# State-space table chunks beside layer 0's MLP: sixteen TensorE visits of one table, or eight of two

## The chip, the core and the metric

The program runs on one core of one Trainium2 chip. The metric is the device time of one execution in microseconds (us). TensorE (PE in the profile) multiplies, VectorE (DVE) and ScalarE (ACT) do the elementwise work, GpSimd (POOL) some more of it, and SyncE (SP) issues the weight loads as DMAs. ScalarE and GpSimd issue DMAs too. The engines run their own instruction streams and meet only at semaphores: a wait holds back everything behind it in the same stream.

## What is computed

A decoder trunk of two layers over 256 tokens of width 2048, all in float32: each layer has a mixer, a cross-attention and an MLP. Layer 1's mixer holds a state-space part, whose step for one group is, in the reference:

```python
lam = lax.complex(jnp.minimum(a_re, -1e-4), a_im)
a_bar = jnp.exp(lam * step)
b_bar = ((a_bar - 1.0) / lam)[..., None] * lax.complex(b_re, b_im)
bu = jnp.einsum('blgc,gpc->blgp', uf, b_bar)
states = associative_scan(combine, (a_seq, bu))      # x_t = a_bar x_(t-1) + bu_t
y = jnp.einsum('blgp,gcp->blgc', states, c_mat).real + d_skip * uf
...
ff = sq_relu_mlp(x, w1, w2)                          # square(relu(x @ w1)) @ w2
```

The kernel turns the scan into chunks of 8 tokens. For that it needs tables that depend on the weights alone: powers of a_bar times b_bar ("E"), c times powers of a_bar ("C"), and the product of both, an 8-token convolution kernel ("K") to which d_skip is added. The 64 groups are made in 16 tables of four groups each, k = 0 to 15, and since they need no activations they are made long before layer 1, beside layer 0's MLP.

## The kernel before

**The MLP.** Layer 0's MLP goes through its 8192 hidden columns in eight steps of 1024. One step is 32 "halves": u = 0 and 1 make the hidden columns (w1), u = 2 and 3 are pair units that multiply them with w2, eight halves i = 0 to 7 each. For a half, ScalarE rounds a slab of weights to whi (L1484), VectorE takes the remainder wlo = raw - whi (L2128), and TensorE multiplies both. whi and wlo are rings of four halves: ScalarE's whi of half t waits until TensorE is done with half t - 4. In the pair units and at the start of the next step VectorE also adds finished blocks to the residual h (add_block, L2176), which is what frees an accumulator bank. TensorE's first half of a next step opens a bank that is freed by the add_block in VectorE's slot i = 1 of that same step.

**The slots of the tables.** The last but one four steps (TAB_CHUNKS) carry the table work. Slots count halves, t = 0 to 127 (32 per step); the slot of half t stands in each stream after that half's own work. For table k, before:

- SP loads its factors at slot 28 + 6k of SP's own stream, behind a wait for the builders of table k - 2.
- VectorE makes the real parts in the four slots from DVE_T[k] = 30 + 6k (L2236 to L2255), and raises s5_re. GpSimd makes the imaginary parts (tt, L3059, and L3277), and raises s5_im. Buffers etab, cz and eb are double (k % 2): a builder of table k waits until table k - 2 has been multiplied and stored.
- TensorE visits at CHUNK_T[k] = 33 + 6k: s5_chunk(k) is four small float32 products (stationary 32 columns, moving 128) into one of the two banks of "at" (L827). The profile shows each visit as eight matmuls.
- ScalarE's slot is four later, 37 + 6k: copy the bank's lower half into ksb (L1594), issue the stores of E (et_d, L1596) and C (ca_d, two of them, L1599), wait for VectorE's two adds (k_sum; VectorE: L2214 and L2217, behind k_part), issue two stores of ksb (k_d, L1602). Then whi of the next half follows.

There is one ksb only: the copy of table k (L1594) waits for k_out, the landing of both k_d stores of table k - 1. At the end GpSimd waits for the last k_out and issues the t_d copies (L3285).

Of the kernel before, what the change touches and what calls it, by code (L numbers as in the profile page):

```python
# [27 lines left out]
ACT = mybir.ActivationFunctionType  # L28
# [3 lines left out]
P = 128  # L32
# [12 lines left out]
G, GC, ST = 64, 16, 64  # L45
# [3 lines left out]
GW = T8 * GC  # L49
# [86 lines left out]
def trunk(nc, x, mem, norm_final, ab_w_in, ab_b_forget,  # L136
# [3 lines left out]
    with ctx:  # L140
# [3 lines left out]
        def sem(name):  # L144
            return ctx.enter_context(nc.semaphore(name))
# [27 lines left out]
        def view(at, n, pattern=None, p=P, **sizes):  # L173
            assert at + n <= A_SIZE
            a = arena[0:p, at:at + n]
            return a.rearrange(pattern, **sizes) if pattern else a
# [12 lines left out]
        etab = view(1024, 1024, "p (b q r w) -> p b q r w", b=2, q=2, r=2)  # L189
# [5 lines left out]
        ksb = view(3200, 240, p=2 * 2 * GC)  # L195
# [7 lines left out]
        cz = [view(at_, 576, "p (q r w) -> p q r w", q=2, r=2) for at_ in (7616, 10240)]  # L203
# [70 lines left out]
        at = ctx.enter_context(nc.psum_tensor("at", [P, 2, NB], F32))  # L274
# [3 lines left out]
        et_d = nc.dram_tensor("et_d", [P, Q, 2, GW], F32, kind="Internal").ap()  # L278
        ca_d = nc.dram_tensor("ca_d", [2, P, Q, GW], F32, kind="Internal").ap()
        k_d = nc.dram_tensor("k_d", [GC, G, 240], F32, kind="Internal").ap()  # L280
# [18 lines left out]
        at_full = sem("at_full")  # L299
# [28 lines left out]
        s5_re, s5_im = sem("s5_re"), sem("s5_im")  # L328
        s5_used = sem("s5_used")
        k_part, k_sum = sem("k_part"), sem("k_sum")  # L330
        f_out, f_in = sem("f_out"), [sem(f"f_in{b}") for b in range(2)]
        et_out, k_out = [sem(f"et_out{b}") for b in range(2)], sem("k_out")
        ca_out = [sem(f"ca_out{b}") for b in range(2)]
        prep_done, tab_zero = sem("prep_done"), sem("tab_zero")
        ksb_zero = sem("ksb_zero")
# [28 lines left out]
        OUT_ORDER = (2, 3, 0, 1)  # L364
        TAB_CHUNKS = (3, 4, 5, 6)
        FACTOR_T, STORE_T = 4, 16
        DVE_T = [32 + 6 * k - 2 for k in range(16)]
        CHUNK_T = [32 + 6 * k + 1 for k in range(16)]
        SIN_T = 29
        X8_T, SCAN_T, Y_T = 25, 39, 53  # L370
        SWAP_T = (49, 51, 52)
# [5 lines left out]
        at_before_tab = at_before_factors + 1  # L377
# [317 lines left out]
        def _(pe):  # L695
            p = Place()
# [119 lines left out]
            def open_at():  # L816
                n = p.n.setdefault("at", 0)
                if n >= 2:
                    pe.wait_ge(at_free[n % 2], n // 2)
                return at[:, n % 2, :]  # L820

            def close_at(last):
                last.then_inc(at_full, 1)
                p.bump("at")

            def mm(o, lhsT, rhs, start=True, stop=True):
                return pe.matmul(o, lhsT, rhs, start=start, stop=stop)  # L827
# [13 lines left out]
            def s5_factors():  # L841

                assert p.n["at"] == at_before_factors
                pe.wait_ge(prep_done, 1)
                bank = open_at()
                for t in range(2):
                    for r in range(2):
                        last = pe.transpose(bank[:, (2 * t + r) * P:(2 * t + r + 1) * P],
                                            pb[:, r, 4 * t:4 * t + 4, :].rearrange("p a b -> p (a b)"), ident[:, :])
                close_at(last)  # L850

            def s5_chunk(k):

                b = k % 2
                pe.wait_ge(s5_re, k + 1)
                pe.wait_ge(s5_im, k + 1)
                bank = open_at()
                for r in range(2):
                    for q in range(2):
                        ln = 2 * GC * (2 * r + q)  # L860
                        last = mm(bank[ln:ln + 2 * GC, 0:GW], eb[:, b, q, r, :], cz[b][:, q, r, 0:GW])
                close_at(last)

            def s5_tables(t):
                if t == FACTOR_T:
                    s5_factors()
                if t in CHUNK_T:
                    assert p.n["at"] == at_before_tab + CHUNK_T.index(t)
                    s5_chunk(CHUNK_T.index(t))

            for u in range(4):
                def after(i, u=u):
# [589 lines left out]
        def _(act):  # L1462
            p = Place()
# [119 lines left out]
            def s5_tables(t):  # L1583

                if t - 4 == FACTOR_T:
                    at_copy(lambda bank: [(fput, bank)])
                if t - 4 not in CHUNK_T:
                    return
                k = CHUNK_T.index(t - 4)
                b = k % 2  # L1590
                n = p.n["at"]
                act.wait_ge(*((k_out, 32 * k) if k else (ksb_zero, 1)))
                act.wait_ge(at_full, n + 1)
                act.activation(ksb[:, 112:240], at[2 * 2 * GC:P, n % 2, 0:GW], ACT.Copy).then_inc(k_part, 1)  # L1594
                p.bump("at")
                act.dma_start(et_d[:, 2 * k:2 * k + 2].rearrange("p q r w -> p (q r w)"),  # L1596
                              etab[:, b].rearrange("p q r w -> p (q r w)")).then_inc(et_out[b], 16)
                for r in range(2):
                    act.dma_start(ca_d[r, :, 2 * k:2 * k + 2], cz[b][:, :, r, GC:]).then_inc(ca_out[b], 16)  # L1599
                act.wait_ge(k_sum, k + 1)  # L1600
                for q in range(2):
                    act.dma_start(k_d.rearrange("c (s k q) w -> k q s c w", s=2, q=2)[k, q],  # L1602
                                  ksb[2 * GC * q:2 * GC * (q + 1), :]).then_inc(k_out, 16)

            for u in range(4):
                def slot(i, u=u):
# [503 lines left out]
        def _(dve):  # L2110
            dve.memset(idle[:, :], 0.0).then_inc(idle_set, 1)
            p = Place()
# [94 lines left out]

            def re_tables(t):

                if t - 4 in CHUNK_T:  # L2210
                    k = CHUNK_T.index(t - 4)
                    n = at_before_tab + k
                    dve.wait_ge(k_part, k + 1)
                    dve.tensor_tensor(ksb[:, 112:240], at[0:2 * 2 * GC, n % 2, 0:GW], ksb[:, 112:240],  # L2214
                                      ALU.add).then_inc(at_free[n % 2], 1)
                    dve.wait_ge(at_free[n % 2], n // 2 + 1)
                    dve.tensor_tensor(ksb[:, 112:112 + GC], ksb[:, 112:112 + GC], skip[:, k, :],  # L2217
                                      ALU.add).then_inc(k_sum, 1)
                part = [(k, t - t0) for k, t0 in enumerate(DVE_T) if 0 <= t - t0 < 4]
                if not part:  # L2220
                    return
                (k, part), = part
                b, q0 = k % 2, 2 * k
                e, tv = etab[:, b, :, 0, :], vtmp3[:, 0:2 * P].rearrange("p (q w) -> p q w", q=2)
                t1 = vtmp2.rearrange("p (q i c) -> p q i c", q=2, i=9)
                t2 = vtmp.rearrange("p (q i c) -> p q i c", q=2, i=9)
                if part == 0:
                    if k == 0:
                        dve.wait_ge(prep_done, 1)
                        dve.wait_ge(tab_zero, 1)  # L2230
                    if k >= 2:
                        dve.wait_ge(at_full, at_before_tab + k - 1)
                        dve.wait_ge(et_out[b], 16 * (k // 2))
                    dve.wait_ge(f_in[b], 32 * (k // 2 + 1))
                    (br, bi), (pbr, pbi) = ((fac[:, b, f, :, r, :] for r in range(2)) for f in range(2))
                    dve.tensor_tensor(e, br, pbr, ALU.mult)  # L2236
                    dve.tensor_tensor(tv, bi, pbi, ALU.mult)
                    (br, bi), (pbr, pbi) = last_parts(q0)
                    dve.tensor_tensor(vlast[:, 0], br, pbr, ALU.mult)
                    link(dve.tensor_tensor(vlast[:, 1], bi, pbi, ALU.mult))  # L2240
                elif part == 1:
                    dve.tensor_tensor(e, e, tv, ALU.subtract)
                    for s in range(2):
                        ln = slice(64 * s, 64 * s + 64)
                        last = dve.tensor_tensor(eb[ln, b, :, 0, s * GC:(s + 1) * GC], vlast[ln, 0], vlast[ln, 1],
                                                 ALU.subtract)
                    link(last)
                elif part == 2:
                    cr, ci, pr_, pi_ = table_parts(s5c, pw, q0, 9)
                    dve.tensor_tensor(t1, cr, pr_, ALU.mult)  # L2250
                    link(dve.tensor_tensor(t2, ci, pi_, ALU.mult))
                else:
                    if k >= 2:
                        dve.wait_ge(ca_out[b], 32 * (k // 2))
                    dve.tensor_tensor(cz[b][:, :, 0, :].rearrange("p q (i c) -> p q i c", i=9), t1, t2, ALU.add)\  # L2255
                       .then_inc(s5_re, 1)
# [1121 lines left out]
```

## Time and profile before

| | us |
|---|---|
| median of 3 runs | 2376.73 (2376.65 to 2376.74) |
| the profiled execution | 2375.98 |
| its span, first to last instruction | 2374.1 |
| TensorE busy | 2361.8 (99%) |
| VectorE, ScalarE, GpSimd busy | 1643.4, 1234.3, 346.3 |
| first and last table visit of TensorE | 948.48, 1205.59 |

A busy TensorE is not one at its peak: its matmuls overlap, so the distance between two starts tells more than a duration. In the tables' steps an ordinary matmul of 512 columns starts 0.225 to 0.23 us after the one before it, and is shown as lasting 0.39.

### The profile page before, as it was taken

What the parts mean: (1) busy time and instruction counts of PE and PEld (TensorE: products, weight loads), DVE (VectorE), ACT (ScalarE), POOL (GpSimd) and SP (SyncE); (2) the same over time, 40 slices, a digit from 0 to 9 for tenths busy, and PEclk for the clock granted to TensorE, in tenths of its full rate; (3) what the DMA queues carried; (4) which work ended last, traced back from release to release, by engine and by line L of the source; (5) the groups of instructions that cost most, each with busy time, mean ns of one, the idle gap of its engine ahead of it and who ended that gap; (6) DMA issues with size and microseconds to landing.
All of it is one profiled execution on the core that took longest, in us unless ns stands there. A gap on an engine that the chain in (4) does not pass through costs nothing.

```text
span 2374.1 us, 31055 instructions
## 1 busy us (share of the span) xinstructions
PE 2361.8 (99%) x12350; PEld 1997.7 (84%) x12350; DVE 1643.4 (69%) x2041; ACT 1234.3 (52%) x1629; POOL 346.3 (15%) x469
## 2 busy tenths in 40 slices
PE   9999999999999999999999999999999999999998
PEld 7888888889888888888888888889888888888887
DVE  5546555556655557888866647566688888888886
ACT  7544445546544444444445445556656555555554
POOL 0033120002264002455510100000000000000001
PEclk9999999999999999999999999999999999999999
DMA  9755564564656566788785768955656756756653
GB/s 357 264 173 188 170 218 163 184 188 145 195 179 198 191 198 212 247 243 253 243 284 186 214 231 237 296 200 155 225 183 220 234 168 221 239 185 205 230 160 142
DMA packets 345082, 499.89 MB, mean 211 GB/s; under 512 B 18904, under 2 KB 184640, under 8 KB 344688
## 3 DMA queue, kind: packets, MB, share of 16 engines
q1 hardware_dynamic: 319792, 471.37, 61.8%
q0 software_dynamic: 3888, 14.02, 1.9%
q10 hardware_dynamic: 21264, 12.59, 1.7%
q8 instruction: 95, 1.56, 0.3%
q14 instruction: 43, 0.35, 0.0%
HBM read 483.06 MB, written 19.08 MB: 212 GB/s over the span
## 4 chain that ended last, share of the span: by engine, by line
PE 95%; DVE 2%; ACT 1%; DMA 1%; issue 0%; ACTq 0%; SPq 0%; DVEq 0%
PE acc L740 15%; PE acc L742 15%; PE acc L741 15%; PE acc L1177 10%; PE acc L1386 9%; PE acc L1185 5%; PE acc L1395 5%; PE acc L1426 2%; PE acc L1425 2%; PE acc L1424 2%; PE at L827 2%; PE tp L803 1%; PE at L1366 1%; PE at L1368 1%; PE at L1369 1%; DVE wlo L2128 1%
## 5 line engine op out<-in xcount | busy, mean ns | idle before, releaser
L2128 DVE TENSOR_TENSOR wlo<-raw,whi 128x1024 fp32r<-128x1024 f32 x592 | 763.1, 1296 | 538.7 <-ACT whi L1484 535.9
L1484 ACT ACTIVATE whi<-raw 128x1024 fp32r<-128x1024 f32 x600 | 630.5, 1059 | 660.6 <-PE acc L742 395.1
L740 PE MATMUL acc<-whi,yt_hi 128*128 128x512 f32 x960 | 378.2, 394 | 0.3 <-DVE h L2176 0.3
L742 PE MATMUL acc<-whi,yt_lo 128*128 128x512 f32 x960 | 374.0, 390 | 0.0
L741 PE MATMUL acc<-wlo,yt_hi 128*128 128x512 f32 x960 | 373.7, 389 | 0.0
L2884 DVE TENSOR_TENSOR wlo<-raw,whi 128x1024 fp32r<-128x1024 f32 x176 | 214.3, 1221 | 80.3 <-ACT whi L2041 74.5
L2041 ACT ACTIVATE whi<-raw 128x1024 fp32r<-128x1024 f32 x168 | 176.0, 1056 | 174.5 <-PE acc L1395 85.6
L740 PE MATMUL acc<-whi,x 128*128 128x512 f32 x672 | 265.8, 396 | 0.0
L1177 PE MATMUL acc<-x,whi 128*128 128x512 f32 x1088 | 262.4, 391 | 0.0
L742 PE MATMUL acc<-whi,x 128*128 128x512 f32 x672 | 261.9, 390 | 0.0
L741 PE MATMUL acc<-wlo,x 128*128 128x512 f32 x672 | 261.7, 389 | 0.0
L3059 POOL TENSOR_TENSOR arena<-arena 128x32 f32<-128x32 f32 (+5 forms) x275 | 197.2, 717 | 357.3 <-DMA arena<-fp_d 179.1
L1177 PEld LDWEIGHTS acc<-x,whi 128*128 128x128 f32 x1088 | 199.6, 188 | 39.3 <-issue 0.8
L740 PEld LDWEIGHTS acc<-whi,yt_hi 128*128 128x128 f32 x960 | 180.3, 188 | 39.3 <-issue 1.8
L1386 PE MATMUL acc<-x,whi 128*128 128x512 f32 x896 | 213.0, 390 | 0.0
L742 PEld LDWEIGHTS acc<-whi,yt_lo 128*128 128x128 f32 x960 | 180.2, 188 | 37.9
L741 PEld LDWEIGHTS acc<-wlo,yt_hi 128*128 128x128 f32 x960 | 180.3, 188 | 36.3
L1386 PEld LDWEIGHTS acc<-x,whi 128*128 128x128 f32 x896 | 166.4, 188 | 33.4
L2030 ACT ACTIVATE whi<-arena 128x1024 fp32r<-128x1024 f32 x98 | 103.2, 1060 | 90.9 <-PE acc L1426 35.0
L740 PEld LDWEIGHTS acc<-whi,x 128*128 128x128 f32 x672 | 126.2, 188 | 26.6 <-issue 1.2
L742 PEld LDWEIGHTS acc<-whi,x 128*128 128x128 f32 x672 | 126.1, 188 | 26.7
L741 PEld LDWEIGHTS acc<-wlo,x 128*128 128x128 f32 x672 | 126.3, 188 | 25.2
(274 smaller groups left out, 3184.6 us busy)
## 6 DMA issues: line engine op xcount, KB each, us to landing
raw<-in_mlp_w SPq DMA_DIRECT2D x228, 1024.0 KB, 5.8
raw<-in_ab_w_in SPq DMA_DIRECT2D x56, 1024.0 KB, 5.1
arena<-in_mlp_w SPq DMA_DIRECT2D x35, 1024.0 KB, 6.5
raw<-in_cd_w_in SPq DMA_DIRECT2D x32, 1024.0 KB, 5.9
raw<-in_ab_w_out SPq DMA_DIRECT2D x16, 1024.0 KB, 5.0
raw<-in_cd_w_out SPq DMA_DIRECT2D x16, 1024.0 KB, 8.3
raw<-in_xa_wkv SPq DMA_DIRECT2D x14, 1024.0 KB, 11.7
raw<-in_xa_wq SPq DMA_DIRECT2D x16, 512.0 KB, 4.5
```

Of the source, the lines that this page charges most:

```text
L740: pe.matmul(a, xh, whi[:, w, kk], start=opens and kk == 0, stop=False)
L741: pe.matmul(a, xh, wlo[:, w, kk], start=False, stop=False)
L742: last = pe.matmul(a, xl, whi[:, w, kk], start=False, stop=closes and kk == 1)
L1177: last = pe.matmul(head(i).rearrange("p (a n) -> p a n", a=2), split_weights(whi, "heads", i)[:, kk, :], x2[:, :, k0 + kk, :], start=i < 4 ...
L1185: last = pe.matmul(head(i)[:, 0:L], split_weights(wlo, "heads", i)[:, kk, :], x2[:, 0, 8 * (i // 4) + kk, :], start=False, stop=i >= 4 and ...
L1386: last = pe.matmul(head(i).rearrange("p (a n) -> p a n", a=2), split_weights(whi, "heads", p.n["half"] + i % 2)[:, kk, :], x2[:, :, 8 * (i ...
L1395: last = pe.matmul(head(i)[:, 0:L], split_weights(wlo, "heads", p.n["half"] + i % 2)[:, kk, :], x2[:, 0, 8 * (i // 4) + kk, :], start=Fals ...
L1484: act.activation(split_weights(whi, kind, p.n["half"] + i), half_weights(raw, kind, i), ACT.Copy)\
L2041: act.activation(split_weights(whi, kind, p.n["half"]), half_weights(raw, kind, i), ACT.Copy)\
L2128: dve.tensor_tensor(split_weights(wlo, kind, n), half_weights(raw, kind, i), split_weights(whi, kind, n).bitcast(F32), ALU.subtract).then_ ...
L2884: dve.tensor_tensor(split_weights(wlo, kind, n), half_weights(raw, kind, i), split_weights(whi, kind, n).bitcast(F32), ALU.subtract).then_ ...
L3059: link(pool.tensor_tensor(o, a, b, op))
```

## The change

TensorE visits eight times instead of sixteen (VISIT_T = 39 + 12v), with tables 2v and 2v + 1 in one visit, at the slot where table 2v + 1 had its own. VectorE's parts of an even table from 2 on start one slot later. ScalarE's stores of E and C keep their slots (37 + 6k), but now wait for the two builders (s5_re, s5_im) instead of for TensorE. The copy, the sums and the k_d stores of a pair (SUM_T) stand at slots 43 + 12v and 45 + 12v, cut off at 127: for the last pair both are 127. GpSimd and SP keep their order.

```diff
--- before.py
+++ after.py
@@ -364,8 +364,10 @@
         OUT_ORDER = (2, 3, 0, 1)
         TAB_CHUNKS = (3, 4, 5, 6)
         FACTOR_T, STORE_T = 4, 16
-        DVE_T = [32 + 6 * k - 2 for k in range(16)]
-        CHUNK_T = [32 + 6 * k + 1 for k in range(16)]
+        DVE_T = [32 + 6 * k - 2 + (k > 0 and k % 2 == 0) for k in range(16)]
+        STORE_TABLE_T = [32 + 6 * k + 5 for k in range(16)]
+        VISIT_T = [32 + 12 * v + 7 for v in range(8)]
+        SUM_T = [min(VISIT_T[k // 2] + 4 + 2 * (k % 2), 127) for k in range(16)]
         SIN_T = 29
         X8_T, SCAN_T, Y_T = 25, 39, 53
         SWAP_T = (49, 51, 52)
@@ -864,9 +866,11 @@
             def s5_tables(t):
                 if t == FACTOR_T:
                     s5_factors()
-                if t in CHUNK_T:
-                    assert p.n["at"] == at_before_tab + CHUNK_T.index(t)
-                    s5_chunk(CHUNK_T.index(t))
+                if t in VISIT_T:
+                    v = VISIT_T.index(t)
+                    assert p.n["at"] == at_before_tab + 2 * v
+                    s5_chunk(2 * v)
+                    s5_chunk(2 * v + 1)
 
             for u in range(4):
                 def after(i, u=u):
@@ -1584,23 +1588,25 @@
 
                 if t - 4 == FACTOR_T:
                     at_copy(lambda bank: [(fput, bank)])
-                if t - 4 not in CHUNK_T:
-                    return
-                k = CHUNK_T.index(t - 4)
-                b = k % 2
-                n = p.n["at"]
-                act.wait_ge(*((k_out, 32 * k) if k else (ksb_zero, 1)))
-                act.wait_ge(at_full, n + 1)
-                act.activation(ksb[:, 112:240], at[2 * 2 * GC:P, n % 2, 0:GW], ACT.Copy).then_inc(k_part, 1)
-                p.bump("at")
-                act.dma_start(et_d[:, 2 * k:2 * k + 2].rearrange("p q r w -> p (q r w)"),
-                              etab[:, b].rearrange("p q r w -> p (q r w)")).then_inc(et_out[b], 16)
-                for r in range(2):
-                    act.dma_start(ca_d[r, :, 2 * k:2 * k + 2], cz[b][:, :, r, GC:]).then_inc(ca_out[b], 16)
-                act.wait_ge(k_sum, k + 1)
-                for q in range(2):
-                    act.dma_start(k_d.rearrange("c (s k q) w -> k q s c w", s=2, q=2)[k, q],
-                                  ksb[2 * GC * q:2 * GC * (q + 1), :]).then_inc(k_out, 16)
+                if t in STORE_TABLE_T:
+                    k = STORE_TABLE_T.index(t)
+                    b = k % 2
+                    act.wait_ge(s5_re, k + 1)
+                    act.wait_ge(s5_im, k + 1)
+                    act.dma_start(et_d[:, 2 * k:2 * k + 2].rearrange("p q r w -> p (q r w)"),
+                                  etab[:, b].rearrange("p q r w -> p (q r w)")).then_inc(et_out[b], 16)
+                    for r in range(2):
+                        act.dma_start(ca_d[r, :, 2 * k:2 * k + 2], cz[b][:, :, r, GC:]).then_inc(ca_out[b], 16)
+                for k in (k for k in range(16) if SUM_T[k] == t):
+                    n = p.n["at"]
+                    act.wait_ge(*((k_out, 32 * k) if k else (ksb_zero, 1)))
+                    act.wait_ge(at_full, n + 1)
+                    act.activation(ksb[:, 112:240], at[2 * 2 * GC:P, n % 2, 0:GW], ACT.Copy).then_inc(k_part, 1)
+                    p.bump("at")
+                    act.wait_ge(k_sum, k + 1)
+                    for q in range(2):
+                        act.dma_start(k_d.rearrange("c (s k q) w -> k q s c w", s=2, q=2)[k, q],
+                                      ksb[2 * GC * q:2 * GC * (q + 1), :]).then_inc(k_out, 16)
 
             for u in range(4):
                 def slot(i, u=u):
@@ -2207,8 +2213,7 @@
 
             def re_tables(t):
 
-                if t - 4 in CHUNK_T:
-                    k = CHUNK_T.index(t - 4)
+                for k in (k for k in range(16) if SUM_T[k] == t):
                     n = at_before_tab + k
                     dve.wait_ge(k_part, k + 1)
                     dve.tensor_tensor(ksb[:, 112:240], at[0:2 * 2 * GC, n % 2, 0:GW], ksb[:, 112:240],
```

On TensorE, at the first two tables (L827 is the helper mm of before; L740 to L742, L1177 and L1185 are the MLP's), before:

```order
L1185 MATMUL acc<-x,wlo 128x256 x8
L827 MATMUL at<-arena 32x128 x4
L1177 MATMUL acc<-x,whi 128x512 x8
L1185 MATMUL acc<-x,wlo 128x256 x8
L1177 MATMUL acc<-x,whi 128x512 x8
L1185 MATMUL acc<-x,wlo 128x256 x16
L1177 MATMUL acc<-x,whi 128x512 x16
L1185 MATMUL acc<-x,wlo 128x256 x16
L1177 MATMUL acc<-x,whi 128x512 x16
L1185 MATMUL acc<-x,wlo 128x256 x8
L827 MATMUL at<-arena 32x128 x4
L1177 MATMUL acc<-x,whi 128x512 x8
```

and now (the same lines carry numbers 2 to 4 higher, mm is L829):

```order
L1189 MATMUL acc<-x,wlo 128x256 x8
L1181 MATMUL acc<-x,whi 128x512 x8
L1189 MATMUL acc<-x,wlo 128x256 x8
L1181 MATMUL acc<-x,whi 128x512 x8
L1189 MATMUL acc<-x,wlo 128x256 x16
L1181 MATMUL acc<-x,whi 128x512 x16
L1189 MATMUL acc<-x,wlo 128x256 x16
L1181 MATMUL acc<-x,whi 128x512 x16
L1189 MATMUL acc<-x,wlo 128x256 x8
L829 MATMUL at<-arena 32x128 x8
L1181 MATMUL acc<-x,whi 128x512 x8
```

Table 0's four products have moved 6 halves down to table 1's, and are one row of eight with them.

On ScalarE, at the last table of all and the start of the next step, before (with what each row waits for):

```order
L1484 ACTIVATE whi<-raw 128x1024 [waits half_used,raw_landed3]
L1484 ACTIVATE whi<-raw 128x1024 [waits half_used]
L1594 ACTIVATE arena<-at 64x128 [waits at_full,k_out]
L1596 DMA et_d<-arena 128x512
L1599 DMA ca_d<-arena 128x2x128 x2
L1602 DMA k_d<-arena 2x16x240 [waits k_sum]
L1602 DMA k_d<-arena 2x16x240
L1484 ACTIVATE whi<-raw 128x1024 [waits half_used,raw_landed0]
L1484 ACTIVATE whi<-raw 128x1024 [waits half_used]
```

and now (L1484 is L1488, L1594 is L1604, L1602 is L1608):

```order
L1488 ACTIVATE whi<-raw 128x1024 [waits half_used]
L1596 DMA et_d<-arena 128x512 [waits s5_im,s5_re]
L1599 DMA ca_d<-arena 128x2x128 x2
L1604 ACTIVATE arena<-at 64x128 [waits at_full,k_out]
L1608 DMA k_d<-arena 2x16x240 [waits k_sum]
L1608 DMA k_d<-arena 2x16x240
L1604 ACTIVATE arena<-at 64x128 [waits at_full,k_out]
L1608 DMA k_d<-arena 2x16x240 [waits k_sum]
L1608 DMA k_d<-arena 2x16x240
L1488 ACTIVATE whi<-raw 128x1024 [waits half_used,raw_landed0]
L1488 ACTIVATE whi<-raw 128x1024 [waits half_used]
```

Between whi of half 127 and whi of half 128 there is now a second copy of a bank, which waits for k_out, with a second pair of k_d stores.

On VectorE at the same place, before (L2214 and L2217 are the sums, L2176 is add_block):

```order
L2128 TENSOR_TENSOR wlo<-raw,whi 128x1024 [waits hi_ready] x4
L2214 TENSOR_TENSOR arena<-at,arena 64x128 [waits k_part]
L2217 TENSOR_TENSOR arena<-arena 64x16 [waits at_free1]
L2128 TENSOR_TENSOR wlo<-raw,whi 128x1024 [waits hi_ready] x2
L2176 SCALAR_TENSOR_TENSOR h<-acc,rstd,h 128x512 [waits half_used]
L2176 SCALAR_TENSOR_TENSOR h<-acc,rstd,h 128x512
L2128 TENSOR_TENSOR wlo<-raw,whi 128x1024 [waits hi_ready]
```

and now (L2128 is L2134, L2176 is L2182):

```order
L2134 TENSOR_TENSOR wlo<-raw,whi 128x1024 [waits hi_ready] x4
L2219 TENSOR_TENSOR arena<-at,arena 64x128 [waits k_part]
L2222 TENSOR_TENSOR arena<-arena 64x16 [waits at_free0]
L2219 TENSOR_TENSOR arena<-at,arena 64x128 [waits k_part]
L2222 TENSOR_TENSOR arena<-arena 64x16 [waits at_free1]
L2134 TENSOR_TENSOR wlo<-raw,whi 128x1024 [waits hi_ready] x2
L2182 SCALAR_TENSOR_TENSOR h<-acc,rstd,h 128x512 [waits half_used]
L2182 SCALAR_TENSOR_TENSOR h<-acc,rstd,h 128x512
L2134 TENSOR_TENSOR wlo<-raw,whi 128x1024 [waits hi_ready]
```

Both pairs of sums stand ahead of wlo of halves 128 and 129, and of the add_block behind them.

## Rows read from the trace of the kernel before

**Rows 1.** The page: the engines' busy time and share of the span.

```profile
PE 2361.8 (99%) x12350; PEld 1997.7 (84%) x12350; DVE 1643.4 (69%) x2041; ACT 1234.3 (52%) x1629; POOL 346.3 (15%) x469
```

**Rows 2.** Waits of TensorE, whole run: waiter, releaser, us in total, times, longest.

```profile
PE acc L740 <- DVE h L2176: 0.3, 1, 0.3
```

**Rows 3.** Timeline, TensorE, last visit: start, us, engine, line, out<-in, count.

```profile
1205.28 0.39 PE L742 MATMUL acc<-whi,yt_lo 128*128 128x512 f32 x1
1205.59 0.43 PE L827 MATMUL at<-arena 128*32 128x128 f32 x8
1205.95 0.50 PE L740 MATMUL acc<-whi,yt_hi 128*128 128x512 f32 x1
1206.29 0.39 PE L741 MATMUL acc<-wlo,yt_hi 128*128 128x512 f32 x1
```

**Rows 4.** Timeline, TensorE, a visit of layer 1 with four such groups.

```profile
1467.02 0.39 PE L742 MATMUL acc<-whi,x 128*128 128x512 f32 x1
1467.34 0.48 PE L827 MATMUL at<-yt_hi,arena 128*32 128x128 f32 x8
...
1468.41 0.50 PE L740 MATMUL acc<-whi,x 128*128 128x512 f32 x1
1468.75 0.40 PE L741 MATMUL acc<-wlo,x 128*128 128x512 f32 x1
```

**Rows 5.** Timeline, TensorE, halves 56 and 58, then the start of the next step.

```profile
1011.89 0.50 PE L740 MATMUL acc<-whi,yt_hi 128*128 128x512 f32 x1 [0.30 <-DVE h L2176]
...
1017.59 0.42 PE L827 MATMUL at<-arena 128*32 128x128 f32 x8
...
1216.98 3.79 PE L1177 MATMUL acc<-x,whi 128*128 128x512 f32 x16
```

**Rows 6.** Timeline, ScalarE, slot 127 (last table) to half 129; ACTq issues DMAs.

```profile
1205.70 1.06 ACT L1484 ACTIVATE whi<-raw 128x1024 fp32r<-128x1024 f32 x1 [1.60 <-PE acc L742]
...
1206.66 0.26 ACT L1594 ACTIVATE arena<-at 64x128 f32<-64x128 f32 x1
...
1208.44 1.20 ACTq L1602 DMA_DIRECT2D k_d<-arena  x2
1209.74 1.06 ACT L1484 ACTIVATE whi<-raw 128x1024 fp32r<-128x1024 f32 x1 [2.82 <-PE acc L742]
```

**Rows 7.** Timeline, VectorE, the same stretch: sums, wlo of half 128, add_block.

```profile
1207.94 0.28 DVE L2214 TENSOR_TENSOR arena<-at,arena 64x128 f32<-64x128 f32 x1
1208.25 0.17 DVE L2217 TENSOR_TENSOR arena<-arena 64x16 f32<-64x16 f32 x1
1210.84 1.22 DVE L2128 TENSOR_TENSOR wlo<-raw,whi 128x1024 fp32r<-128x1024 f32 x1 [2.42 <-ACT whi L1484]
...
1213.98 1.40 DVE L2176 SCALAR_TENSOR_TENSOR h<-acc,rstd,h 128x512 f32<-128x512 f32 x2
```

**Rows 8.** Timeline, GpSimd: the end of a table, and t_d behind the last k_out.

```profile
1178.88 10.10 POOL L3059 TENSOR_TENSOR arena<-arena 128x256 f32<-128x256 f32 x9 [5.86 <-DMA ca_d<-arena]
1189.06 0.89 POOL L3277 TENSOR_TENSOR arena<-arena 128x288 f32<-128x288 f32 x1
1216.37 6.17 POOL L3285 DMA_DIRECT2D t_d<-k_d  x8 [26.42 <-DMA k_d<-arena]
```

**Rows 9.** The view of the tile ca_d: its DMAs, issue to landing.

```profile
DMA to landing us min/median/max: 3.4/6.4/10.1
```

**Rows 10.** Timeline, TensorE's last matmul of the program.

```profile
2365.08 0.39 PE L764 MATMUL acc<-whi,yt_lo 128*128 128x512 f32 x1
```

**Rows 11.** Windows behind it: PE, PEld, DVE, ACT, POOL busy (count), PEclk, DMA.

```profile
2368.00:2370.00 2.00, 0.00 (x0) 0.00 (x0) 1.69 (x4) 1.15 (x1) 0.00 (x0) 0.95 0.00 0
2370.00:2372.00 2.00, 0.00 (x0) 0.00 (x0) 0.00 (x0) 0.00 (x0) 0.00 (x0) 0.50 0.72 297
```

**Rows 12.** Windows, L827 at the program's start: PE busy (count), PEld busy (count).

```profile
1.20:3.20 2.00, 2.00 (x5) 0.90 (x6) 1.00 0.60 166
3.20:5.20 2.00, 2.00 (x8) 0.92 (x7) 1.00 1.05 389
```

## The prediction

> **What bounds the kernel.** I read the page first: TensorE is busy for 99% of the span [rows 1]. Then the view of waits, for TensorE alone: in the steps with table work it waits once, 0.3 us, for an add_block of VectorE [rows 2], and the timeline puts that at the start of half 56 [rows 5]. So a change can only act in three ways: through what a table visit costs on TensorE itself, through that one wait, or by making VectorE or ScalarE late enough to stop TensorE. For the last I read, engine by engine, the place where the order changed most: the last table, slot 127.
>
> **Visits merged: a gain.** Starts of ordinary matmuls are 0.227 us apart. Round the last visit the starts run 1205.28, 1205.59, 1205.95, 1206.29 [rows 3]: 1.01 us where two ordinary distances take 0.45, so a visit of one table costs 0.56. How much of that is per visit and how much per table no table visit shows, but layer 1's visits do, with four groups of the same shape: 1467.02 to 1468.75 is 1.73 [rows 4], less 0.45 is 1.28. Each further group adds (1.28 - 0.56) / 3 = 0.24. A pair in one visit then costs 0.80 instead of 1.12, and eight pairs save 8 x 0.32 = **2.5 us**. If the second table cost its whole inner distance of 0.36, it would be 8 x 0.20 = 1.6. If it cost 0.22 (the inner distance left if the longer first and last ones are set apart), 2.7. I take 2.5, since the four-group visit holds the same waits and the same change of bank. All of it is on the path, because TensorE waits for nothing else.
>
> **VectorE one slot later for even tables: 0.3 gained.** The 0.3 us before half 56 come from the sums of table 3 and the parts of table 4 standing ahead of an add_block. Part 0 of table 4 (the longest) moves behind slot 54, the wlo of half 56 comes earlier, and the wait should go. Bound 0, I take **0.3**.
>
> **The last visit: a loss.** The pairs' sums are two slots apart, except the last pair's, whose two stand in slot 127. There is one ksb, so the second copy waits until the first k_d stores have landed, and behind it on ScalarE's stream stands whi of half 128. Worked out with the rows of the same place:
> - The first k_d pair is issued at 1208.44 for 1.20, to 1209.64 [rows 6]. It doesn't come earlier or later than before, since VectorE's sums at 1207.94 follow its wlo [rows 7].
> - Landing: GpSimd's t_d copies, which wait for the same semaphore, start at 1216.37 [rows 8], so 6.7 after the issue ended at most. By the ca_d stores' median of 6.4 from the issue [rows 9], the second store (issued some 0.6 before 1209.64) lands at 1215.4. I take 1215.9, between the two.
> - Then copy 0.26 [rows 6], sums 0.48 (1207.94 to 1208.42 [rows 7]), stores 1.20, and some 0.2 in hand-overs: whi of half 128 starts at 1218.04 instead of 1209.74 [rows 6].
> - VectorE's wlo starts 1.10 behind it [rows 6, 7]: 1219.1. Two wlo (1.22 each) and the add_block (1.40) [rows 7] end at 1222.9. Before, that add_block ended at 1215.38.
> - TensorE's half 128 needs this add_block's bank. It started at 1216.98 [rows 5]; a visit longer by 0.24 makes it 1217.2. The cover before was 1.6 us, now TensorE stands still for 1222.9 - 1217.2 = **5.7 us**.
>
> The unknown is the landing. With the least of a store's landings, 3.4, it is 1212.4 and the stall 2.2. With the most, 10.1, it is 1219.1 and the stall 8.9 [rows 9].
>
> **The clock: a loss on top.** A stall of that length is new to this trace. What it does to the clock is bounded by the program's two ends. After the last matmul ends at 2365.47 [rows 10], the granted clock is 1.00, then 0.95 in 2368 to 2370, then 0.50 [rows 11]: 0.95 is 0.1 x 2 us at half rate, so it fell from 2.4 to 1.2 GHz at 2369.8, 4.3 us after TensorE had stopped. A stop of 5.7 is longer. At the start 5 matmuls lie in the first 2 us and 8 in the next 2 [rows 12]; with 0.43 us each at first and half of it later, the low rate lasts for 3.2 us of work and loses 1.6. The bounds are 0 and twice that. I take **1.6**. The Trainium skill's page "TensorE: Matmul & The Clock Gate", Part 1, has the same rule, throttled by default and released by sustained activity; by the end of this trace it agrees, and no row shows a fall in mid-kernel.
>
> **Edits taken at nothing.** The odd table of a pair other than the last: its copy comes two slots after the even one's stores. From the visit: 4.05 to the end of the k_d issue (1205.59 to 1209.64), 6.3 to land, 1.9 for copy, sums and stores, then 1.06, 1.22 and 1.40 for the next half and its block. That is 16.0, and TensorE comes to that bank after a 0.8 visit and six halves of 12 x 0.227, 17.1. So 1 us of cover at slots 57, 81 and 105, where a block is handed over, and more elsewhere; VectorE's table parts there can eat it. I take 0, bound 3 x 1.2. GpSimd now starts both tables of a pair behind one visit: a table lasts 11.1 (1178.88 to 1189.95 [rows 8]), two 22, and visits are 12 halves apart. 66 halves lie between 1017.59 and 1205.59 [rows 3, 5], 2.85 each, so 34 us. ScalarE's new wait for the builders comes 6 halves, 17 us, behind the visit that frees an even table's buffers, where its builder needs some 12; the odd one has 34 for 23. SP's factor load of the next even table comes about 11 us behind it, so SP may wait up to 1 us ahead of weight loads that are issued eight halves early. Both at 0.
>
> **Sum.** -2.5 - 0.3 + 5.7 + 1.6 = +4.5 us. The profiled execution of 2375.98 would take 2380.5; the median lies 0.75 above it, so 2376.73 + 4.5 = **2381.2**.
>
> **The rivals.**
> - *The stall without the fall of the clock.* The sum without 1.6 is +2.9, 2379.6. For it: the stop is only 1.4 us longer than the 4.3 us after which the clock fell [rows 10, 11], and a landing 1.5 us sooner undoes it.
> - *The k_d stores land quickly, and the change is faster than before.* They are 30 KB each behind a few larger stores. It decides at a stall of 2.8, that is a landing at 1213.0, 3.4 after the issue. With the least landing [rows 9] the sum is -2.5 - 0.3 + 2.2 = -0.6, 2376.1. Against it: this very store took until close to 1216.37 [rows 8]. The Trainium skill's page "DMA: Bandwidth & Descriptors", Anatomy of one DMA, gives some 2 us of fixed cost and next to nothing for so few bytes; by it the stall would be about 0.9 and the time 2374.8, but the trace doesn't agree (3.4 is its least).
> - *Longer landings, or VectorE late in the middle too.* Landing 10.1 makes the sum +7.7, and the three places with 1 us of cover add up to 3.6 where landings are long: 2385 and over.
>
> **How the numbers follow.** Forecast 0.50, stall without clock 0.28, quick landing 0.10, long 0.12. The range, 2377.5 to 2385.0, takes in the first two with their bounds and half of each of the others. A measurement of this kernel tells about 0.2%, 4.75 us: slower means over 2381.5. A good 0.4 of the forecast's cases lie above it (0.22), half the clock-less ones' upper bound reaches it (0.06), and the long ones do (0.12): slower 0.40. Faster than 2372.0 needs a gain no term holds: 0.02. The rest, 0.58, is no change.
>
> **What would show it.** Right: TensorE has one long idle time, before half 128 at about 1217, ended by VectorE's h (L2182), with the second copy (L1604) and its k_d stores some 8 us behind the first; a granted clock below 1 for a few us behind it; eight visits of 16 matmuls costing 0.80. Wrong: no idle time there (the landing is quicker), idle time at halves 58, 82 or 106, ScalarE waiting for GpSimd ahead of et_d, or visits that cost 1.1.

## The result

| | before | changed | |
|---|---|---|---|
| median | 2376.37 us (9 runs, 2375.07 to 2376.93) | 2383.58 us (9 runs, 2383.19 to 2384.50) | ratio 1.0029 [1.002, 1.0037] |
| span of the profiled execution | 2374.1 | 2382.4 | |

The changed kernel is 7.2 us slower, 0.3%. By the prediction's own line of 2381.5 that is slower, to which it gave 0.40; it held no change to be likelier (0.58). The first view to read is again that of TensorE's waits, of the changed kernel (its add_block is L2182, its sums of hidden columns are L2518); in [rows 2] there was one line for these steps:

```profile
PE acc L1181 <- DVE h L2182: 5.9, 2, 5.4
PE acc L712 <- ACT whi L1488: 1.5, 2, 1.3
...
PE acc L742 <- DVE h L2182: 1.0, 1, 1.0
PE acc L742 <- DVE arena L2518: 0.8, 1, 0.8
```

One wait of 5.4 us is new, and three short ones (0.46, 0.98 and 0.84). The L712 line is the start of the program and not of the change: another profile of the same kernel (the run called "the changed kernel again" below) shows 0.3 there. It matters only for the two profiled spans: a matmul that starts at 15.76 before starts at 16.75 here, so 1.0 of the 8.3 us between the spans lies there, and 7.3 remain. TensorE's timeline, at the last visit and at the start of the next step (it answers to [rows 3] and the last of [rows 5]):

```profile
1205.88 0.39 PE L744 MATMUL acc<-whi,yt_lo 128*128 128x512 f32 x1
1206.20 0.65 PE L829 MATMUL at<-arena 128*32 128x128 f32 x16
1206.77 0.50 PE L742 MATMUL acc<-whi,yt_hi 128*128 128x512 f32 x1
1207.11 0.40 PE L743 MATMUL acc<-wlo,yt_hi 128*128 128x512 f32 x1
...
1217.57 0.39 PE L744 MATMUL acc<-whi,yt_lo 128*128 128x512 f32 x1
1223.38 5.74 PE L1181 MATMUL acc<-x,whi 128*128 128x512 f32 x16 [5.42 <-DVE h L2182]
```

A visit of two tables takes 1.23 us from start to start where two ordinary distances take 0.45: 0.78. The first matmuls behind the stop take 5.74 us for sixteen, 3.79 before [rows 5]. Why TensorE stops, read from the bottom up: the timelines of ScalarE and of VectorE in the same kernel (they answer to [rows 6] and [rows 7]).

```profile
1209.05 1.20 ACTq L1608 DMA_DIRECT2D k_d<-arena  x2
1216.44 0.28 ACT L1604 ACTIVATE arena<-at 64x128 f32<-64x128 f32 x1 [8.27 <-DMA k_d<-arena]
1217.27 1.19 ACTq L1608 DMA_DIRECT2D k_d<-arena  x2
1218.56 3.90 ACT L1488 ACTIVATE whi<-raw 128x1024 fp32r<-128x1024 f32 x4 [1.84 <-PE acc L744]
```

```profile
1216.75 0.28 DVE L2219 TENSOR_TENSOR arena<-at,arena 64x128 f32<-64x128 f32 x1 [7.74 <-ACT arena L1604]
1217.07 0.17 DVE L2222 TENSOR_TENSOR arena<-arena 64x16 f32<-64x16 f32 x1
1219.65 2.36 DVE L2134 TENSOR_TENSOR wlo<-raw,whi 128x1024 fp32r<-128x1024 f32 x2 [2.41 <-ACT whi L1488]
1221.92 1.40 DVE L2182 SCALAR_TENSOR_TENSOR h<-acc,rstd,h 128x512 f32<-128x512 f32 x2
```

The add_block ends at 1223.32, TensorE starts at 1223.38. It waited for two wlo, they for whi, whi for the second pair of k_d stores, those for the sums, the sums for the second copy, and the copy for table 14's stores: it starts 6.2 us after their issue ended at 1210.25, so they had landed by then.

The windows of the changed kernel show the clock (columns: PE, PEld, DVE, ACT, POOL busy, the granted clock, the DMA share and GB/s):

```profile
1216.00:1219.00 3.00, 1.96 (x9) 1.30 (x7) 0.45 (x2) 0.72 (x2) 0.00 (x0) 1.00 0.02 6
1219.00:1222.00 3.00, 0.00 (x0) 0.00 (x0) 2.35 (x3) 3.00 (x4) 1.05 (x2) 0.74 0.04 15
1222.00:1225.00 3.00, 1.62 (x4) 1.33 (x5) 3.00 (x5) 0.45 (x1) 3.00 (x5) 0.50 0.81 233
1225.00:1228.00 3.00, 3.00 (x10) 2.38 (x9) 1.91 (x3) 0.00 (x0) 2.13 (x3) 0.62 0.90 243
1228.00:1231.00 3.00, 3.00 (x22) 2.79 (x21) 0.00 (x0) 0.83 (x1) 0.00 (x0) 1.00 1.04 391
```

0.74 over 3 us is 1.56 us at half rate, so the clock fell from 2.4 to 1.2 GHz at 1220.4, 2.5 us after the last matmul's end. 0.62 is 2.28 us, so it rose at 1227.3, 3.9 us after TensorE had taken up work. That is 1.95 us lost, 5.74 less 3.79. These figures are one execution's. In the second profile of this kernel the windows put the fall 4.0 us after the last matmul's end and the rise 5.6 us after the restart, and the same sixteen matmuls take 6.54 us: 2.75 lost.

### The profile page after: what moved, and what is told of

The parts are those of the page before. It is cut to its first block, busy times and chain, and to the rows that moved or that the text cites. A ratio compares the mean times of both kernels' runs of the same rounds, so it can differ in the third digit from the quotient of the medians.

```text
span 2382.4 us, 31071 instructions
## 1 busy us (share of the span) xinstructions
PE 2362.2 (99%) x12350; PEld 1999.8 (84%) x12350; DVE 1629.1 (68%) x2041; ACT 1235.0 (52%) x1629; POOL 335.5 (14%) x469
## 3 DMA queue, kind: packets, MB, share of 16 engines
q8 instruction: 95, 1.56, 0.3%
## 4 chain that ended last, share of the span: by engine, by line
PE 93%; DVE 3%; ACT 2%; DMA 1%; issue 1%; ACTq 0%; SPq 0%; DVEq 0%
PE acc L742 15%; PE acc L744 14%; PE acc L743 14%; PE acc L1181 10%; PE acc L1390 9%; PE acc L1189 5%; PE acc L1399 4%; PE acc L1428 2%; PE acc L1429 2%; PE acc L1430 2%; PE at L829 2%; PE tp L805 1%; PE at L1370 1%; PE at L1372 1%; PE at L1373 1%; DVE wlo L2134 1%
## 5 line engine op out<-in xcount | busy, mean ns | idle before, releaser
L2134 DVE TENSOR_TENSOR wlo<-raw,whi 128x1024 fp32r<-128x1024 f32 x592 | 752.2, 1277 | 548.4 <-ACT whi L1488 545.6
L1488 ACT ACTIVATE whi<-raw 128x1024 fp32r<-128x1024 f32 x600 | 630.0, 1058 | 638.7 <-PE acc L744 401.1
L742 PE MATMUL acc<-whi,yt_hi 128*128 128x512 f32 x960 | 377.8, 394 | 1.8 <-DVE h L2182 1.0
L2889 DVE TENSOR_TENSOR wlo<-raw,whi 128x1024 fp32r<-128x1024 f32 x176 | 214.2, 1221 | 80.3 <-ACT whi L2047 74.5
L742 PE MATMUL acc<-whi,x 128*128 128x512 f32 x672 | 265.8, 396 | 0.0
L3064 POOL TENSOR_TENSOR arena<-arena 128x32 f32<-128x32 f32 (+5 forms) x275 | 178.8, 650 | 368.9 <-DMA arena<-fp_d 179.0
L742 PEld LDWEIGHTS acc<-whi,yt_hi 128*128 128x128 f32 x960 | 180.3, 188 | 40.1 <-DVE h L2182 1.4
L742 PEld LDWEIGHTS acc<-whi,x 128*128 128x128 f32 x672 | 126.2, 188 | 26.5 <-issue 1.2
```

The source lines that it names most:

```text
L742: pe.matmul(a, xh, whi[:, w, kk], start=opens and kk == 0, stop=False)
L1488: act.activation(split_weights(whi, kind, p.n["half"] + i), half_weights(raw, kind, i), ACT.Copy)\
L2134: dve.tensor_tensor(split_weights(wlo, kind, n), half_weights(raw, kind, i), split_weights(whi, kind, n).bitcast(F32), ALU.subtract).then_ ...
L2889: dve.tensor_tensor(split_weights(wlo, kind, n), half_weights(raw, kind, i), split_weights(whi, kind, n).bitcast(F32), ALU.subtract).then_ ...
L3064: link(pool.tensor_tensor(o, a, b, op))
```

## The experiments

Two theories for the end: **L**, the last landing stops TensorE and the stop lowers the clock; **S**, two rounds of copy, sums and stores are too much for slot 127 whatever lands when. For the three short waits: the landings again, or **R**, the round trip between ScalarE and VectorE. Twelve runs, each beside runs of the kernel before on the same chip. The medians of these lie from 2376.8 to 2377.7, and all their single runs but one (2434.3) from 2375.0 to 2380.8; most versions spread less, so differences between the versions are tighter than those against the kernel before. "Under the changed kernel" is against its 2383.58; measured again, on the chip of two of the versions, it gave 2383.43.

**A second ksb for the last table alone.**

```diff
-        ksb = view(3200, 240, p=2 * 2 * GC)
+        ksbs = [view(at_, 240, p=2 * 2 * GC) for at_ in (3200, 3936)]
...
-                    n = p.n["at"]
-                    act.wait_ge(*((k_out, 32 * k) if k else (ksb_zero, 1)))
+                    n, ksb = p.n["at"], ksbs[k == 15]
+                    act.wait_ge(*((k_out, 32 * k) if 0 < k < 15 else (ksb_zero, 1)))
```

> The changed kernel, but table 15 (the last) has a ksb of its own, so its copy does not wait for the landing of table 14's k_d stores; all other tables share one ksb as in the change. Theory L (the last landing stops TensorE, and the stop lowers the clock): the idle time before half 128 (5.4 us in the changed kernel) and the 3.9 us of work at half the clock (2 us lost) both go, the three short waits at halves 48, 96 and 120 stay: about 7.4 us faster than the changed kernel, within 1 us of the kernel before. Rival S (ScalarE and VectorE are late at slot 127 because of two rounds of copy, sums and stores, whatever the landing): the idle time shrinks by 1 to 2 us only.

2375.77 us, ratio 0.9995 [0.9986, 1.0004] to before: 7.8 under the changed kernel. (One of its twelve executions took 13593.9 us, for a reason that the record doesn't show; the others took 2375.3 to 2376.7.) TensorE has no idle time at half 128 and the granted clock stays at 1.00; the three short waits stand (0.46, 0.83, 0.98). L holds, S falls: two rounds in one slot are covered.

**Two ksb, for all tables** (`ksbs[k % 2]`, and `k_outs[k % 2]` with 32 * (k // 2)).

> The changed kernel with two ksb, one for even and one for odd tables, each with its own landing semaphore: no copy waits for the stores of its own pair. Theory L for the end as in the run with a second ksb for table 15 only. For the short waits at halves 48, 96 and 120 two theories: if the landings make ScalarE late there too, they go, and the time is 2.5 to 3 us under the kernel before; if it is the second round of copy, sums and stores two slots after the first (ScalarE waiting for VectorE's sums), they stay, and the time is that of the run with a second ksb for table 15 only.

2375.15, ratio 0.9994 [0.9985, 1.0003], and again beside later runs:

> The version with two ksb as before, again, to stand beside the one with later stores on the same chip: 1 to 2 us under the kernel before, waits of 0.83 and 0.98 us at halves 48 and 120.

2375.44, ratio 0.9992 [0.9983, 1.0001]. The waits at halves 48 and 120 stay at 0.83 and 0.98, the one at 96 goes. So the landings made the one, and something else the other two: the expectation had them all go or all stay.

**The changed kernel again**, in the same session.

> The changed kernel itself on the same chip: 7 us over the kernel before, 8.5 over the version with two ksb.

2383.43, ratio 1.0027 [1.0018, 1.0036], idle time 5.1 before half 128: the result repeats. The clock's part does so only roughly, as said above (2.75 us lost against 1.95).

**TensorE kept busy during the stop.**

```diff
+                if t == 127:
+                    pe.wait_ge(at_free[0], (at_before_tab + 14) // 2 + 1)
+                    for _ in range(12):
+                        mm(at[0:32, 0, 0:L], ident[:, 0:32], idle)
```

> The changed kernel with 12 extra small products of TensorE (24 matmul records of 0.215 us, 5.2 us in all) between half 127 and half 128, into a bank nobody reads, in the time in which it stands idle. If the idle time is what lowers the clock, TensorE stays at 2.4 GHz, the first sixteen matmuls of half 128 take 3.8 us instead of 5.7, and the whole is about 2 us faster than the changed kernel. If the clock falls for another reason, the time is that of the changed kernel. If the filling itself runs past the release, up to 0.5 us are lost.

2381.10, ratio 1.0019 [1.001, 1.0028]: 2.5 under the changed kernel. Its timeline, TensorE:

```profile
1216.78 5.37 PE L829 MATMUL at<-arena,ident 128*32 128x256 f32 x24
1222.11 3.96 PE L1185 MATMUL acc<-x,whi 128*128 128x512 f32 x16
```

Half 128 still begins 5.4 us late, since its bank comes no sooner, but its sixteen matmuls take 3.96 instead of 5.74 or 6.54, at a granted clock of 1.00. So the idle time itself lowered the clock, and products that nobody reads buy it back. The 2.5 us lie between the two clock losses seen.

**Stores of E and C behind the k_d stores in slot 127** (the block of stores is moved below the sums' loop for t == 127).

> The changed kernel, but in slot 127 the three stores of table 15 (E and C, 512 KB) are issued behind the two copies, sums and k_d stores instead of ahead of them. In the changed kernel k_d stores with such stores just ahead on the same queue land 5.2 to 6.2 us after their issue, those without after 2.9 to 3.8. If the stores ahead make the landing long, table 14's lands about 3 us sooner and is issued up to 0.5 sooner, but the three stores then stand between it and whi of half 128 (1.4 us): idle time about 3.5 instead of 5.4, and with no fall of the clock or a shorter one: 2 to 4 us faster than the changed kernel. If the landing is long because of the weight loads, the time is 1 us slower than the changed kernel.

2385.44, ratio 1.0035 [1.0022, 1.0048]: 1.9 over the changed kernel. ScalarE's timeline:

```profile
1208.06 1.21 ACTq L1611 DMA_DIRECT2D k_d<-arena  x2
1215.19 0.27 ACT L1607 ACTIVATE arena<-at 64x128 f32<-64x128 f32 x1 [8.65 <-DMA k_d<-arena]
```

The issue ends at 1209.27, the copy starts 5.9 later. The stores ahead on the queue are not what makes the landing long. They only move in front of whi, and the idle time grows to 6.7. My first guess was wrong here. The DMA view by short stretches shows what the landing waits for, since only the k_d stores are on ScalarE's queue in this run: between 1209.3 and 1212.8 that queue moves no packet and SyncE's moves 896, of the weight load; the k_d packets run from 1213.2 to 1214.8, and the load's last ones end by 1213.4. In the changed kernel they run from 1214.4 to 1216.0, with most of the load through by 1214.5. The clock is at 1.2 GHz here too: it falls 2.7 us after the last matmul's end and rises 2.8 us after the restart, and the sixteen matmuls take 5.24 us, 1.45 lost.

**One weight load cut to an eighth**, the one issued 0.4 us ahead of the k_d stores. This version leaves out seven eighths of that load, so it computes something else and only its time counts.

```diff
...
+                        rows = 128 if cut and i == 3 else 1024
-                        sp.dma_start(raw[:, i].rearrange("p a (b n) -> p (a b) n", b=2),
+                        sp.dma_start(raw[:, i].rearrange("p a (b n) -> p (a b) n", b=2)[:, 0:rows // 128],
...
```

> The changed kernel, but one weight load, that for halves 134 and 135 (issued 0.5 us ahead of table 14's k_d stores, 1 MB, landing 0.6 us ahead of them), brings only its first 128 of 1024 rows, so part of layer 0's MLP is computed with stale weights. If the k_d stores land late because they queue behind this load's packets, table 14's land 2.5 to 3.5 us after their issue instead of 6.2, the idle time before half 128 is 2 to 3 us instead of 5.4, the clock does not fall, and the time is 4.5 to 5.5 us under the changed kernel. If a store with nothing but itself takes that long, nothing changes.

2377.65, ratio 1.0006 [0.9996, 1.0015]: 5.9 under the changed kernel. ScalarE and then TensorE:

```profile
1207.87 1.21 ACTq L1609 DMA_DIRECT2D k_d<-arena  x2
1211.25 0.28 ACT L1605 ACTIVATE arena<-at 64x128 f32<-64x128 f32 x1 [4.29 <-DMA k_d<-arena]
```

```profile
1218.20 3.96 PE L1182 MATMUL acc<-x,whi 128*128 128x512 f32 x16 [1.42 <-DVE h L2183]
```

The copy comes 2.2 us after the issue's end instead of 6.2, the idle time is 1.4 and the clock stays at 1.00. With the packets of the run before this one: a store of 30 KB lands no sooner than the megabyte of weights that was issued just ahead of it on another queue. By what order the packets of the two queues are served, no run shows.

**Both sums of a pair in one slot**, with two ksb: both copies, both sums, then four k_d stores behind one wait.

> The version with two ksb, and the two sums of every pair in one slot (43 + 12v): ScalarE copies both banks, VectorE makes both sums, then ScalarE issues the four k_d stores; one wait for VectorE per pair instead of two. Theory R (the waits at halves 48 and 120 come from the second round of copy and sums two slots after the first): they go, 1.8 us of idle time, and the time is about 2 us under the version with two ksb alone, 3.5 to 4 us under the kernel before. Rival V (they come from VectorE having table parts to do there anyway): they stay, and nothing changes against two ksb alone.

2376.34, ratio 0.9999 [0.999, 1.0008], 1.2 over two ksb alone, so neither theory's forecast came. The waits at halves 48 and 120 shrink to 0.35 and 0.60, but three others come, at 56, 80 and 104 (0.61, 0.53, 0.52), as the timeline reads because ScalarE now issues four stores in one piece:

```profile
1004.37 2.43 ACTq L1610 DMA_DIRECT2D k_d<-arena  x4
1006.90 2.02 ACT L1488 ACTIVATE whi<-raw 128x1024 fp32r<-128x1024 f32 x2 [3.32 <-issue]
```

R as I put it, the second round alone, falls: one long block of ScalarE's stream is as bad as two short ones.

**The same without VectorE's shift** (`DVE_T = [32 + 6 * k - 2 for k in range(16)]`).

> The same with VectorE's parts of even tables at the slots of the kernel before (30 + 6k), so without the shift by one slot. If the shift is what took the 0.3 us wait at half 56 away, it comes back here, and VectorE waits 1 to 2 us more for TensorE's visit at the start of an even table. If the wait went for another reason, the time is that of the version with one round, within 0.5 us.

2384.28, ratio 1.0031 [1.0019, 1.0042], 7.9 over the version with the shift. TensorE waits three times, where a bank's owner comes late, and VectorE waits three times for TensorE's visit (2.3 us in all, about as expected). What was not expected is the price:

```profile
PE acc L742 <- DVE h L2184: 2.6, 1, 2.6
PE acc L742 <- DVE arena L2520: 1.7, 1, 1.7
PE acc L1181 <- DVE arena L2520: 1.7, 1, 1.7
```

The 0.3 us that I gave the shift is far too little here: with two sums in slot 43 + 12v, part 0 of the next table one slot ahead of them costs 1.7 to 2.6 us at each of halves 56, 80 and 104. These waits make some 4 of the 7.9 us (its profiled span is 2379.7 against 2376.2). The profiled execution is one of the fast ones: the three of seven executions with a mean granted clock of 0.999 took 2381.4 to 2382.1, and the four with 0.997 or 0.998 took 2384.3 to 2385.8. So in those four the clock probably falls as well; where, no profile shows.

**The other half of the change alone**: the kernel before, sixteen visits, stores ahead of the copy and waiting for the builders.

> The kernel before, sixteen visits, with the other half of the change alone: ScalarE issues a table's stores of E and C ahead of the copy, and waits for the two builders first. The stores were issued 0.4 us behind the start of the slot's whi; they come a little sooner, the copy comes 1 us later, hidden behind VectorE's wlo. All theories: no change, within 0.5 us of the kernel before.

2377.78, ratio 1.0003 [0.9994, 1.0012]. No change that can be told, though its profile has one wait more, 1.2 us at half 104 for VectorE (L2515). There the issue of the two C stores, now ahead of the copy, lasts 3.54 us (1.05 to 2.15 at the other tables), so the copy comes 3.8 us later than before and the sums 1.9.

**ScalarE's k_d stores one slot later**, two ksb: copy in slot s, wait and stores in slot s + 1, behind the next whi.

```diff
...
+                for k in (k for k in range(16) if min(SUM_T[k] + 1, 127) == t):
+                    ksb = ksbs[k % 2]
                     act.wait_ge(k_sum, k + 1)
...
```

> The version with two ksb, and ScalarE's k_d stores of a table (with their wait for VectorE's sums) one slot behind its copy, so behind the next whi; only the last pair keeps both in slot 127. If the waits at halves 48 and 120 come from ScalarE standing still until VectorE's sums are made, while whi waits behind it, they go, and the time is 2 us under the version with two ksb alone and 3.5 to 4 us under the kernel before. If VectorE itself has too much to do there, they stay.

**2372.51**, ratio 0.998 [0.9971, 0.9989]: faster than both kernels, and 2.9 under two ksb in the same session. In the table steps TensorE has no wait left. ScalarE's timeline at tables 0 and 1, first of the changed kernel, then of this one:

```profile
975.99 0.26 ACT L1604 ACTIVATE arena<-at 64x128 f32<-64x128 f32 x1
979.91 1.19 ACTq L1608 DMA_DIRECT2D k_d<-arena  x2
981.21 2.96 ACT L1488 ACTIVATE whi<-raw 128x1024 fp32r<-128x1024 f32 x3 [4.96 <-PE acc L1181]
```

```profile
974.11 0.26 ACT L1604 ACTIVATE arena<-at 64x128 f32<-64x128 f32 x1
974.62 1.06 ACT L1488 ACTIVATE whi<-raw 128x1024 fp32r<-128x1024 f32 x1 [0.26 <-PE acc L1189]
977.58 1.19 ACTq L1610 DMA_DIRECT2D k_d<-arena  x2
```

The sums come late because VectorE has a wlo, a part of a table and a hidden block ahead of them. VectorE in the changed kernel, from that wlo on:

```profile
976.63 1.65 DVE L2134 TENSOR_TENSOR wlo<-raw,whi 128x1024 fp32r<-128x1024 f32 x1
978.20 1.23 DVE L2526 TENSOR_TENSOR yt_lo<-arena,yt_hi 128x512 fp32r<-128x512 f32 x1
979.36 0.27 DVE L2219 TENSOR_TENSOR arena<-at,arena 64x128 f32<-64x128 f32 x1
...
982.37 1.23 DVE L2134 TENSOR_TENSOR wlo<-raw,whi 128x1024 fp32r<-128x1024 f32 x1 [1.75 <-ACT whi L1488]
```

In the changed kernel whi waits behind the stores that wait for the sums, and VectorE then waits for whi: both stand still in turn. Here whi goes first.

**The same in the kernel before**, sixteen visits and one ksb.

> The kernel before, sixteen visits and one ksb, with ScalarE's k_d stores one slot behind the copy (the last table's stay in slot 127). If merging visits is what the best version (two ksb, eight visits, later stores: 2372.5) gains, this one keeps all but the 0.3 us wait at half 56: 0.3 us under the kernel before. If the later stores are the gain, it comes within 1 us of 2372.5.

2375.46, ratio 0.9993 [0.9984, 1.0002]. TensorE has no wait in the table steps here either. 2372.51 with eight visits against 2375.46 with sixteen is 2.95 us, in two sessions on two chips; each against the kernel before beside it (4.4 and 2.2 under it), the difference is 2.2. The two also differ in the second ksb, in VectorE's shift and in the order of the stores, but with no wait left in either, the merging is what remains; by the timelines it is 8 x (2 x 0.56 - 0.78) = 2.7. So the expectation's first case, merging as the gain, holds, but its "0.3 us under the kernel before" can't be told from the 2.2 measured: its interval runs from 0.9984 to 1.0002.

## Why the prediction was right, and where not

The time lies in the range (2377.5 to 2385.0), the direction and the mechanism are those of the forecast, and 7.2 came where 4.5 was said.

| step | predicted | measured |
|---|---|---|
| merged visits | -2.5 (0.80 a pair) | -2.7 (0.78 a pair), -2.2 to -2.95 between two versions |
| wait at half 56 | -0.3 | gone, -0.3 (with what idle time leaves out, -0.5) |
| stop before half 128 | +5.7 | idle 5.42; 5.6 from start to start |
| the clock | +1.6 | +1.95 (+2.75 in the second profile) |
| VectorE and ScalarE late in mid-stretch | 0 | idle 2.3 in three places; 2.8 from start to start |
| sum | +4.5 | +7.2 |

(The measured column is one profiled execution's: its terms add up to 7.2, the difference of the spans without the program's start is 7.3, that of the medians 7.2. "Start to start": a matmul is shown as 0.39 us long and the next starts after 0.227, so each idle time hides 0.16 more.)

- *The last visit* went link by link as worked out: landing said 1215.9, the copy came at 1216.44; whi 1218.04 against 1218.56, the release 1222.9 against 1223.3, with a start that was half a microsecond later throughout. That the landing came out so well is in part luck. The view of ca_d [rows 9] takes in 32 loads of layer 1 beside the 32 stores; the stores alone have 3.4, 5.6 and 9.0. With their median the lower bound would have been 1214.6 and the middle 1215.5, 0.9 before the copy.
- *The clock* fell in all three profiles with a stop of over 5 us, 2.5, 4.0 and 2.7 us after the last matmul's end, where I took 4.3 from the program's end, and stayed at the low rate for 3.9, 5.6 and 2.8 us of work instead of 3.2. So the rival "stall without the fall" had less for it than its 0.28, and the 1.6 lies within the losses seen, 1.45 to 2.75, without being tied to any of them: it came from the program's start, where the granted clock is shown as 1.00 [rows 12] and only the distances between matmuls are longer. The run with 1.4 us of idle time showed no fall.
- *"Edits taken at nothing"* is the step that failed. I looked for late VectorE at halves 58, 82 and 106, counting one chain from landing to block. The waits came at 48, 96 and 120, where a landing wasn't even the cause in two of three. The chain I left out is that k_sum's wait on ScalarE holds whi back while VectorE works through its own stream, twice within two slots, and that the delay was not made up in the three halves until the next bank changes hands.
- *GpSimd and the stores' new wait* cost nothing, as said: ScalarE never waited for a builder. SyncE waited longer for VectorE ahead of the factor loads than the 1 us worked out, up to 6.7 us (1.3 before), but in the table steps ScalarE never waited for a weight load.
- *The quick landing* was not the case. The cut load shows what it needed, 2.2 us with an eighth of the load ahead of it, and that the rival's time would not have come even so: with 1.4 us of idle time the kernel took 2377.65, not less than before, because the short waits stood.
- *The Trainium skill's* 2 us of fixed cost ("DMA: Bandwidth & Descriptors", Anatomy of one DMA), given there for DMAs that GpSimd issues, is close to what this case shows for ScalarE's stores without a whole weight load in flight: 2.2 us with the load cut, and 2.5 from the end of table 15's k_d issue (1218.46) to the t_d copies (1220.95) in the changed kernel. Behind a whole weight load it is a third of the 6.2.

## What to carry to other kernels

When steps are merged or clipped to a last slot, look at the last instance by itself: here seven pairs had two slots between their halves, and the eighth had none, and a single-buffered tile turned that into a DMA's landing on the path. A wait for another engine belongs behind the work that third parties are waiting for; moving it one slot later was worth as much as the merging, with eight visits (with sixteen, where there was only 0.3 us of waiting to take, no change could be told). And a long stop of TensorE costs more than its length: in the three profiles with a stop of 5.1 to 6.7 us the clock took between a fifth and a half on top, with a stop of 1.4 us nothing.

## What was not expected of the hardware

- A 30 KB store from ScalarE's queue landed within 5.9 to 6.2 us of its issue with a 1 MB load of SP's queue just ahead, its packets moving only when the load's last ones did, and within 2.2 us with that load cut to 128 KB. Taking 512 KB of stores on its own queue out of its way took 0.3 us off.
- The clock fell 2.5, 2.7 and 4.0 us after TensorE's last matmul in three mid-kernel stops, two of them of the same kernel, and 4.3 us after it at the program's end [rows 10, 11]; it came back after 3.9, 2.8 and 5.6 us of work. Small float32 products into an unread bank kept it up.
